# Moving Hyena's inverse transforms, splitting the key and query norm, and finishing a last branch bank by bank, in a two-stack mixer network on one core

## The reference, cut to what matters

```python
def first_block(x, ...):                       # twice (DEPTH = 2), L = 256 tokens, D = 1024
    for i in range(DEPTH):
        x = x + 0.5 * _swiglu(_rmsnorm(x), gate, up, down)
        q, k, v, z, beta_logit, alpha, hy_in = split(_rmsnorm(x) @ w_in[i])
        # delta rule: _dwconv, silu, q and k through _l2norm, chunks of 64, two directions
        o_dn = _deltanet_group(q, k, v, z, beta_logit, alpha, ...)
        # Hyena: v, x1, x2 = split(_dwconv(hy_in)); twice zz = gate * (_fft_conv(zz) + skip * zz); _rmsnorm
        o_hy = _hyena_group(hy_in, ...)
        x = x + concatenate([o_dn, o_hy]) @ w_out[i]
        x = x + 0.5 * _swiglu(_rmsnorm(x), ...)
    return _rmsnorm(x)

def second_block(x, ...):                      # twice
    for l in range(DEPTH):
        proj = rmsnorm(x) @ w_in[l]            # attention, retention, a short convolution, 3 * D gates
        y = (gates[0] * (o_da @ w_branch_da[l]) + gates[1] * (o_ret @ w_branch_ret[l])
             + gates[2] * (o_sc @ w_branch_sc[l]))
        x = x + y @ w_out[l]
        x = x + gated_ffn(rmsnorm(x))
```

## Time and profile before

| | |
|---|---|
| time, median of 3 runs | 2065.13 us (2063.52 to 2068.04) |
| span of the profiled execution | 2060.0 us |
| PE busy | 2015.8 us, 98% of the span |
| PEld busy | 1847.1 us, 90% |
| DVE busy | 951.1 us, 46% |
| ACT busy | 1039.2 us, 50% |
| POOL busy | 1491.8 us, 72% |
| mean granted clock of TensorE | 0.998 of full |

### The profile page before, as it was taken

How to read it: one execution, slowest core, us unless ns; L and a number is a source line. 1 busy time by engine, 2 the same in 40 slices (tenths; PEclk the granted TensorE clock), 3 DMA queues, 4 the chain that set the end, 5 groups by cost and what they waited for, 6 DMA issues and landing times.

```text
span 2060.0 us, 37047 instructions
## 1 busy us (share of the span) xinstructions
PE 2015.8 (98%) x15795; PEld 1847.1 (90%) x15795; DVE 951.1 (46%) x1587; ACT 1039.2 (50%) x1549; POOL 1491.8 (72%) x652
## 2 busy tenths in 40 slices
PE   7999999999999999999999999999999999999998
PEld 7998778989989997778899989999999899999997
DVE  3660766435204550766344203745476028345750
ACT  5443446564436443446464437456644374556442
POOL 6789445458887788445368887768788877687886
PEclk9999999999999999999999999999999999999999
DMA  6755333035555655233135565545555555455553
GB/s 219 235 179 201 102 111 115 23 124 184 186 193 177 216 182 196 94 103 103 44 123 184 185 225 163 164 144 184 164 181 183 195 156 161 145 189 167 184 185 123
DMA packets 250965, 329.10 MB, mean 160 GB/s; under 512 B 9008, under 2 KB 225586, under 8 KB 250418
## 3 DMA queue, kind: packets, MB, share of 16 engines
q1 hardware_dynamic: 250802, 326.73, 48.9%
HBM read 325.66 MB, written 1.05 MB: 159 GB/s over the span
## 4 chain that ended last, share of the span: by engine, by line
PE 60%; DVE 3%; issue 1%; ACT 1%; POOL 0%; DVEq 0%; ACTq 0%
PE psA L406 12%; PE psA L407 12%; PE psA L408 12%; PE psB L407 5%; PE psB L406 5%; PE psB L408 5%; PE psB L1931 1%; PE psA L1773 1%; PE psA L2101 0%; PE psA L1774 0%; PE psA L1779 0%; PE psA L2103 0%; DVE small L1515 0%; PE psB L2091 0%; PE psA L1885 0%
## 5 line engine op out<-in xcount | busy, mean ns | idle before, releaser
L1017 POOL TENSOR_TENSOR w_lo<-raw,w_hi 128x1024 fp32r<-128x1024 f32 x600 | 1459.1, 2450 | 535.0 <-ACT w_hi L593 533.4
L406 PE MATMUL psA<-xT_hi,w_lo 128*128 128x256 f32 x3168 | 909.1, 287 | 4.1 <-POOL w_lo L1017 2.2
L407 PE MATMUL psA<-xT_lo,w_hi 128*128 128x256 f32 x3168 | 896.2, 283 | 0.0
L408 PE MATMUL psA<-xT_hi,w_hi 128*128 128x256 f32 x3168 | 896.2, 283 | 0.0
L593 ACT ACTIVATE w_hi<-raw 128x1024 fp32r<-128x1024 f32 x600 | 630.1, 1052 | 383.0 <-PE psB L408 251.4
L406 PEld LDWEIGHTS psA<-xT_hi,w_lo 128*128 128x128 f32 x3168 | 607.5, 192 | 15.2 <-issue 10.3
L407 PEld LDWEIGHTS psA<-xT_lo,w_hi 128*128 128x128 f32 x3168 | 607.7, 192 | 3.4 <-issue 3.4
L408 PEld LDWEIGHTS psA<-xT_hi,w_hi 128*128 128x128 f32 x3168 | 607.5, 192 | 0.0
L1163 DVE TENSOR_TENSOR hT_lo<-hfull,hT_hi 128x256 fp32r<-128x256 f32 x132 | 242.8, 1874 | 1.3 <-ACT hT_hi L726 0.6
L407 PE MATMUL psB<-w_lo,hT_hi 128*128 128x512 f32 x528 | 210.7, 399 | 0.0
L406 PE MATMUL psB<-w_hi,hT_lo 128*128 128x512 f32 x528 | 208.2, 394 | 0.4 <-issue 0.4
(11 more groups left out here) (440 smaller groups left out, 2290.2 us busy)
## 6 DMA issues: line engine op xcount, KB each, us to landing
raw<-in_w_in SPq DMA_DIRECT2D x78, 1024.0 KB, 5.2
raw<-in_ffn_w_gate SPq DMA_DIRECT2D x44, 1024.0 KB, 5.3
raw<-in_ffn_w_up SPq DMA_DIRECT2D x44, 1024.0 KB, 5.4
raw<-in_ffn_w_down SPq DMA_DIRECT2D x44, 1024.0 KB, 4.8
raw<-in_w_ffn_in SPq DMA_DIRECT2D x44, 1024.0 KB, 5.0
raw<-in_w_ffn_out SPq DMA_DIRECT2D x22, 1024.0 KB, 4.8
raw<-in_w_out SPq DMA_DIRECT2D x16, 1024.0 KB, 4.8
raw<-in_w_branch_da SPq DMA_DIRECT2D x4, 1024.0 KB, 4.9
```

Source lines behind the costliest of these rows:

```text
L406: nc.tensor.matmul(o, a_lo, b_hi, start=start, stop=False, skip_group_check=skip)
L407: nc.tensor.matmul(o, a_hi, b_lo, start=False, stop=False, skip_group_check=skip)
L408: return nc.tensor.matmul(o, a_hi, b_hi, start=False, stop=stop, skip_group_check=skip)
L1017: nc.gpsimd.tensor_tensor(split_half(w_lo, n, kind), raw_half(n, kind), split_half(w_hi, n, kind).bitcast(F32), ALU.subtract)\
```

## The change: what it does

Three edits. In the first stack both inverse transforms come one projection later in TensorE's list (the first after `turn_hyena(l, 5)`, behind projection 15, the second behind projection 20), the forward transform behind projection 16, and the steps of DVE and ACT that go with them move as well: the spectral products of the second round from i = 15, 16 to 16, 17, the gates from 14, 19 to 15, 20, ACT's squares of `zz` from 20 to 21, Ln from 21 to 22, Exp from 22 to 23, the scaling of `zz` from 23 to 24. `qk_sums` and `turn_back` stay where they were. Second, Exp and the multiplication by `rr` are each cut in two, keys first, and the key products wait for the keys' part alone. Third, `last_branch` goes through the banks of branch 2 once, with half 56 and half 57 for each bank, and releases both halves in the last bank.

```diff
@@ ACT, stack1_mixer @@
-                    if i == 20:
+                    if i == 21:
                         for rb in range(RB):
                             act.wait_ge(s1["zz"].sem, s1["zz"].due(l, 2 + rb + 1))
                             A(ytmp[:, rb, :], zz[:, rb, :], ACT.Square, accum_out=g(288 + rb, 289 + rb)).then_inc(s1["hy_ss"].sem, 1)
-                    if i == 21:
                         A(stat[:, 46:47], eps, ACT.Ln, bias=eps)
+                    if i == 22:
                         act.wait_ge(s1["hy_ss"].sem, s1["hy_ss"].due(l, 2))
                         act.wait_ge(s1["qk_mm"].sem, s1["qk_mm"].due(l, 1))
...
-                    if i == 22:
+                    if i == 23:
                         act.wait_ge(ch.sem, ch.step(l))
-                        A(rr[:, :, :], rr[:, :, :], ACT.Exp, scale=-0.5).then_inc(s1["qk_root"].sem, 1)
+                        for v in (slice(4, 8), slice(0, 4)):
+                            A(rr[:, v, :], rr[:, v, :], ACT.Exp, scale=-0.5).then_inc(s1["qk_root"].sem, 1)
                         A(g(292, 294), g(292, 294), ACT.Exp, scale=-0.5).then_inc(ch.sem, 1)
-                    if i == 23:
+                    if i == 24:
@@ DVE, stack1_projections @@
-                    if i in (11, 12, 15, 16):
-                        spectral_product(l, i // 15, (i + 1) % 2)
-                    if i in (14, 19):
-                        hyena_gate(l, i // 19, 0)
-                        hyena_gate(l, i // 19, 1)
+                    if i in (11, 12, 16, 17):
+                        spectral_product(l, i // 16, (i + i // 16 + 1) % 2)
+                    if i in (15, 20):
+                        hyena_gate(l, i // 20, 0)
+                        hyena_gate(l, i // 20, 1)
@@ DVE, deltanet @@
-                dve.wait_ge(s1["qk_root"].sem, s1["qk_root"].due(l, 1))
-                V.tensor_tensor(qkvT[:, 0:8, :], qkvT[:, 0:8, :], rr[:, :, :], ALU.mult).then_inc(s1["qk_norm"].sem, 1)
+                for n, v in enumerate((slice(4, 8), slice(0, 4))):
+                    dve.wait_ge(s1["qk_root"].sem, s1["qk_root"].due(l, n + 1))
+                    V.tensor_tensor(qkvT[:, v, :], qkvT[:, v, :], rr[:, v, :], ALU.mult).then_inc(s1["qk_norm"].sem, 1)
@@ TensorE, stack1_projections @@
                     if i == 14:
                         turn_hyena(l, 4)
-                        hyena_inverse(l, 0)
                     if i == 15:
                         turn_hyena(l, 5)
+                        hyena_inverse(l, 0)
+                    if i == 16:
                         hyena_spectrum(l, 1)
-                    if i == 19:
+                    if i == 20:
                         hyena_inverse(l, 1)
@@ TensorE, key_products @@
-                pe.wait_ge(s1["qk_norm"].sem, s1["qk_norm"].due(l, 1))
...
+                    if c == 0:
+                        pe.wait_ge(s1["qk_norm"].sem, s1["qk_norm"].due(l, n // 2 + 1))
@@ TensorE, new, called in place of the loop for branch 2 @@
+            def last_branch(l, k):
+
+                for i in range(2):
+                    pe.wait_ge(lo_done[1].sem, lo_done[1].due(l, 50 + k + i + 1))
+                for m, b in enumerate(bank_order[2]):
+                    pe.wait_ge(s2["br"].sem, s2["br"].due(l, bank_order[0].index(b) + 1))
+                    for i in range(2):
+                        hi, lo = split_half(w_hi, 50 + k + i, "B"), split_half(w_lo, 50 + k + i, "B")
+                        for c in (2 * b, 2 * b + 1):
+                            v = slice(c * P, (c + 1) * P)
+                            ins_ = product(psA[:, b, (c % 2) * L:(c % 2 + 1) * L], hi[:, v], lo[:, v], xT_hi[:, k + i, :],
+                                           xT_lo[:, k + i, :], i == 0 and c % 2 == 0, i == 1, skip=True)
+                        if m == 3:
+                            ins_.then_inc(half_used[1].sem, 1)
+                    if m < 3:
+                        ins_.then_inc(s2["br_mm"].sem, 1)
```

More of the change, by code:

```diff
@@ L2288, in stack2_mixer @@
                     x_hi, x_lo = (daT_hi, daT_lo) if r == 0 else (xT_hi, xT_lo)
+                    if r == 2:
+                        last_branch(l, k)
+                        continue
                     for i in range(n):
```

6 lines of the change are left out of this document (2 added, 4 removed).

## The result

| | before | changed |
|---|---|---|
| time, median of 4 runs each | 2064.32 us (2062.93 to 2068.04) | 2052.86 us (2051.23 to 2053.96) |
| ratio, with its 95% interval | | 0.9941 [0.9927, 0.9955] |
| span of the profiled execution | 2060.0 us | 2052.0 us |
| mean granted clock in it | 0.998 | 0.999 |

The changed kernel is 11.5 us faster. The forecast was 2054.9 us in a range of 2051.5 to 2059.5, so it is 2.0 us too high and the range holds the time. A run of the changed kernel takes 2.0 us more than its span (2053.96 for 2052.0).

The account below looks back on a forecast made before the run. TensorE's list was taken to bound the kernel. Span 2060.0 - 11.0 (first stack) + 0.8 (last branch) = 2049.8; with the median 5.1 above the span, 2054.9 us, range 2051.5 to 2059.5.

Parts of the forecast that it names:

- The first edit's 2.7 us per layer: First inverse transform, first stack: its wait for Ysp goes, gaining 2.7 us per layer, between 2.5 and 2.9.
- The new wait at `turn_back`: At turn_back, TensorE newly waits 1.6 us per layer for ACT's zz, because the norm steps start later.
- The keys' wait gone: At the key products, the wait of 2.77 us for DVE goes, 2.9 per layer from start to start.
- The order of keys and queries worth little: Second edit: keys first gains little by itself; even an undivided product would end near 347.4, when the key products start.
- The clock of the key products: Key products run at full clock, 3.8 us instead of 5.30, another 1.5 us per layer.
- The masks covered by 0.7 us: Delta rule's first products: POOL's masks done about 358.1, TensorE there at 358.8; cover 0.7 us where there were 5.8.
- The third edit: 0.4 us lost per layer in waits: Last branch: ACT's round of half 60 delays yT_hi and yT_lo, losing 0.4 us per layer, 0.8 for both.
- The first stack's 11.0 us: First stack: 2.7 + 2.9 - 1.6 + 1.5 = 5.5 us gained per layer, 11.0 for both.
- The median: Whole kernel: the median of the runs lies 5.1 us above the span, giving 2054.9 us.
- the weights' stream would take back what the mixers gain: Rival, after the mixers: the weights' stream sets the pace and nothing moves, 2065 us; chance 0.07.
- The slower case: Rival, at turn_back: ACT's chain makes the wait pass 6.7 us per layer and eat all gains, say 2073 us; chance 0.03.
- the faster case: Rival: last branch gains 0.4 instead of losing 0.4, or turn_back's wait is under 1 us: 2052.5 us; chance 0.07.

Follow-up runs that it names:

- early norm steps: Changed kernel without its third edit, with Ln, Exp and the scaling of zz back at their old places in ACT's list: 2055.14 us, ratio 0.9964.
- POOL's queue moved by two halves: Changed kernel without its third edit, norm steps at their old places, ACT's rounds of halves 93 and 94 behind the silu of v: 2054.98 us, ratio 0.9959.
- late rounds: Changed kernel with ACT's rounds of halves 60 and 61 behind the first and second yT_hi: 2049.61 us, ratio 0.9936.
- POOL quiet: Kernel before with ACT's rounds of halves 93 and 94 moved behind the silu of v: 2061.85 us, ratio 0.9995.

## Why the prediction held, point by point

**The first edit's 2.7 us per layer: right.** No wait is left at the inverse transforms, none came at the forward ones.

**The new wait at `turn_back`: right in place and cause, 1.28 us per layer in place of 1.6.** The changed kernel runs 288.72 - 288.15 = 0.57 us later in its own trace, so its `turn_back` at 346.83 compares with a forecast of 346.5 + 0.57 = 347.1. ACT's chain was walked 0.3 us too long, and its table load cost 1.30 us (340.94 to 342.24), as the trace of before had it.

**The keys' wait gone: right; the duration behind it wrong.** Halves of 1.76 us were forecast from the 3.51 of the earlier trace rows. A half takes 1.14, because 1.24 of those 3.51 us were POOL's turn. The step that failed is the reading of a duration as the operation's own cost. A second miss hid it: DVE starts at 344.20, some 0.6 us later than the forecast has it, because two fills (1.11 us) stand ahead of the product in its list. It did no harm, because the keys were ready at 345.34 and TensorE came at 347.76; with early norm steps the same operation costs 2.9 us a half on average, and nearly half of the gain is gone.

**The order of keys and queries worth little: right beside the first edit** (0.9936 without it). Alone its median was 1.7 us lower, which the text did not foresee; the trace puts it down to one stall of 2.8 us broken into two and no fall of the clock.

**The clock of the key products: right, on a ground that does not hold.** They won 1.73 us per layer instead of 1.5. The text relied on the pair with 2.54 us idle having kept the clock; the same pair lost it in both layers of two other executions. The conclusion has better support after the fact: in the seven profiles that have the wait of 1.2 to 1.3 us at `turn_back`, the clock is full behind all fourteen.

**The masks covered by 0.7 us: right that they are covered, wrong in how.** The text let TensorE wait for all four masks of level 0 and had them done at 358.1. They are done at 359.01, because DVE's 128x512 product meets them and they take 3.48 us instead of 2.67; by the text's reckoning this would be 0.1 us behind TensorE, at 358.91. But the products go mask by mask, and the first was ready at 356.22, so 2.7 us of cover were there. With POOL's queue moved by two halves it was used up, and 1.8 us per layer were lost.

**The third edit: 0.4 us lost per layer in waits, right** (3.7 against 2.9, through ACT's round, as the late rounds showed). (The text's own step to 1433.05 is loose: four operations of 0.7 us from 1430.45 end at 1433.25. It plays no part, since ACT decides.) What the sum lacked is the clock: a stall of 1.86 us there can be followed by the half clock, and both profiles of the changed kernel have it in one layer, at 1.7 us. The text weighed the clock for the mixer and not for this place. This is why the spans differ by 8.0 and not by the 10.2 of the sum.

**The first stack's 11.0 us: near the 10.4 measured, in part by luck.** From the transposes behind projection 14 to the first product with a mask, layer 0 took 364.34 - 288.15 = 76.2 us and takes 358.91 - 288.72 = 70.2, and layer 1 the same: 6.0 us per layer, 11.9 for both, where the text has 5.5 (the wait at `turn_back` is 0.3 shorter and the clock gives 0.2 more). Of these, 0.6 us had gone ahead of the first mixer and 1.0 went between the two mixers, where the waits for `w_lo` grew from 0.4 to 1.6 us.

**The median: in the range, with errors that in part cancel.** The prediction took 5.1 us between span and median for start and end. Start and end take 1.7 to 1.9 us in the 45 other executions of the kernel before and 2.0 in the changed one; so the profiled execution of before took about 2060.0 + 1.8 = 2061.8 us, 2.5 below its median, at the low end. Against the changed kernel's profiled execution, the span was forecast 2.2 us too low (2049.8 for 2052.0) and start and end 3.1 too high; that execution, in turn, is the slowest of its four, 1.1 above their median. Together 3.1 - 2.2 + 1.1 = 2.0. The same terms take the 8.0 us of the spans to the 11.5 of the medians: 8.0 + 2.5 + 1.1 - 0.2 = 11.4.

What sets the executions of before apart goes with the clock: the 13 with a mean granted clock of 0.998 took 2061.1 to 2062.8 us, the 22 with 0.997 took 2062.4 to 2066.3, and the 10 with 0.995 or 0.996 took 2064.3 to 2068.2. Of the 49 executions of kernels with the first edit, 46 have 0.999 or 1.0. So the first edit removes waits, and with them falls of the clock, of which the one profile of before had only two. That these falls make the whole spread of before is not shown; the executions without a trace give only their mean clock.

What decides whether a given stall is followed by the half clock stays open; the runs show only that the stall's length alone doesn't.

**The rivals.** That the weights' stream would take back what the mixers gain did not come true: its waits grew by 1.0 us of 11.5. The slower case needed a wait of 6.7 us at `turn_back`; it was 1.28. The 2052.5 of the faster case follows from neither of its conditions: the branch alone gives 2054.9 - 1.6 = 2053.3, the wait alone, shorter by 0.6 per layer, 2053.7, and both together 2052.1. Neither came true, although the median of 2052.86 lies next to it.

## What to carry to other kernels

Read a duration beside what the neighbour engine does at that moment before you scale it: a DVE product with two inputs in SBUF ran 1.14 us where POOL did not get in first, and 2.45 to 3.3 where it did. When a release moves to the end of a longer loop, look for the engine that waits for it ahead of something more urgent: here a round stood in front of `yT_hi`, and moving it took the wait from 1.86 to 1.0 us, below the 1.45 of before. And a stall of about 2 us on TensorE should be priced twice, as itself and as the clock that may fall behind it, and compared over several executions.

## What the runs showed of the hardware

**DVE and POOL take turns.** The same product of 128 x 2048 took 3.51 us with a subtraction of POOL under way, 2.22 with POOL idle and 2.27 with POOL's subtraction coming later; halves of it took 1.14, and 2.45 to 3.3 behind POOL, and POOL's subtraction 3.34 instead of 2.4. Whichever started first ran at its own length, and the other stood until it had ended (POOL 0.2 us less than that). The Trainium skill, SBUF — State Buffer, section "SBUF: two separate sides", says that the port pair shared by the two engines is an exclusive lock for a whole instruction, and that a DVE operation with two SBUF inputs takes it against a GpSimd operation that reads SBUF. The trace agrees: POOL ends at 349.80, and DVE's second half, next in its list since 347.59, ends one half later, at 350.89.

**The half clock is not settled by the stall's length.** Ahead of the inverse transform, 2.54 us: full clock in both layers of the profile of before and of the second edit alone, half clock in both layers of two other executions. Ahead of the key products, 2.77 us: half in all four places of two executions. Ahead of the output projection, 1.86 us: half in one layer and full in the other in two executions of the changed kernel, the other way round the second time; full in both layers with the third edit alone and with the second undone. Two stalls of 1.80 and 1.25 us with 16 matmuls between them: full. 1.45 and 1.0 us at the branch: full in every profile.

**A stall with no releaser in the profile.** In layer 1 of the delta rule TensorE stands for 1.0 to 2.1 us in every profile of the study, the kernel before included (1.59 us), and the profile names nothing that it waits for. None of the edits touches the code there, and yet the stall is 1.05 us in one kernel and 2.14 in another. In the two executions of the changed kernel it was 1.60 and 1.59 us, and a shorter one of the same kind in layer 0 was 1.32 and 0.96. The half clock stood behind it at 1.80 us (POOL quiet) and at 1.85 us (early norm steps), and not at 1.80 (both together) nor at 2.14 (the second edit alone). So differences of a microsecond between two single profiles, and a fall of the clock more or less, need not come from what the edit was meant to do. Its cause is open.
